# HGRN2 and mixture-of-experts trunk on one core: gate granules beside the outputs' norm, and the experts' first turning and row sums in other places

## The reference, cut to what matters

```python
def hgrn2(h, w_in, lb, o_norm_g, w_out):           # layer 1, 256 frames, 8 heads of 128
    q, f, i, g = jnp.split(h @ w_in, 4, axis=-1)
    forget = lb + (1.0 - lb) * jax.nn.sigmoid(f)
    k = 1.0 - forget;  q = jax.nn.silu(q)
    # S_t = diag(f_t) S_{t-1} + (1-f_t) i_t^T,  o_t = S_t^T q_t
    ...
    o = rms_norm(o.reshape(bsz, s, C_HEADS, C_HEAD_DIM), o_norm_g...).reshape(bsz, s, C_WIDTH)
    return (o * jax.nn.silu(g)) @ w_out

def moe_swiglu(h, w_router, b_router, w_gu, w_down):   # 8 experts, top 2, 3584 hidden
    ...
    for e in range(N_EXPERTS):
        out = out + gates[..., e:e + 1] * swiglu(h, w_gu[e], w_down[e])
    return out
```

## Time and profile before

| | us |
|---|---|
| median of 3 runs | 1519.24 |
| lowest, highest | 1518.81, 1524.04 |
| profiled execution | 1523.19 |
| its span | 1521.4 |
| PE, DVE, ACT busy in it | 1482.4, 1248.0, 1001.9 |

### The profile page before, as it was taken

One profiled execution on the slowest core, in us unless ns is written; L12 is line 12 of the kernel. 1 busy time (PEld: TensorE's weight loads), 2 busy tenths in 40 slices (PEclk: granted clock), 3 DMA queues, 4 the chain that ended last, 5 costly groups with the idle time before them and its releaser, 6 DMA issues.

```text
span 1521.4 us, 23764 instructions
## 1 busy us (share of the span) xinstructions
PE 1482.4 (97%) x6931; PEld 1231.4 (81%) x6931; DVE 1248.0 (82%) x1591; ACT 1001.9 (66%) x1267; POOL 36.3 (2%) x43
## 2 busy tenths in 40 slices
PE   8999999999988899999999999999999999999988
PEld 6877888788887688888888888888888888888876
DVE  6996545584867899988998899899989989898995
ACT  6555444375233577777877777787777778778762
POOL 1000000000000000000000000000000000000000
PEclk9999999999989999999999999999999999999999
DMA  7666655555331899999999999999999999999960
GB/s 271 214 216 220 198 189 178 177 167 184 111 111 42 281 402 386 349 376 410 336 378 410 363 349 409 381 334 411 390 324 409 405 336 386 401 348 381 410 240 28
DMA packets 124743, 453.09 MB, mean 298 GB/s; under 512 B 13968, under 2 KB 13968, under 8 KB 124704
## 3 DMA queue, kind: packets, MB, share of 16 engines
q1 hardware_dynamic: 119952, 435.25, 76.6%
q0 software_dynamic: 4752, 17.34, 3.2%
HBM read 444.14 MB, written 8.39 MB: 297 GB/s over the span
## 4 chain that ended last, share of the span: by engine, by line
PE 91%; DVE 6%; ACT 1%; issue 1%; DMA 0%; DVEq 0%; SPq 0%; ACTq 0%
PE PS L447 28%; PE PS L449 28%; PE PS L448 28%; DVE w_lo L1279 2%; PE PS L835 2%; PE PS L689 2%; DMA raw<-in_w_in_ab 0%; ACT w_hi L940 0%; DVE xT_lo L1349 0%; PE PS L497 0%; PE PS L801 0%; PE PS L515 0%; ACT xT_hi L955 0%; PE PS L583 0%; DVE x L1337 0%
## 5 line engine op out<-in xcount | busy, mean ns | idle before, releaser
L1279 DVE TENSOR_TENSOR w_lo<-raw,w_hi 128x1024 fp32r<-128x1024 f32 x486 | 568.7, 1220 | 33.2 <-ACT w_hi L940 31.0
L447 PE MATMUL PS<-w_hi,xT_hi 128*128 128x512 f32 x1424 | 566.5, 398 | 8.9 <-DVE w_lo L1279 4.0
L449 PE MATMUL PS<-w_lo,xT_hi 128*128 128x512 f32 x1424 | 557.9, 392 | 0.0
L448 PE MATMUL PS<-w_hi,xT_lo 128*128 128x512 f32 x1424 | 556.9, 391 | 0.0
L940 ACT ACTIVATE w_hi<-raw 128x1024 fp32r<-128x1024 f32 x486 | 489.6, 1061 | 71.5 <-PE PS L449 44.5
L1279 DVE TENSOR_TENSOR w_lo<-SC,w_hi 128x1024 fp32r<-128x1024 f32 x340 | 392.0, 1219 | 10.6 <-ACT w_hi L940 9.0
L940 ACT ACTIVATE w_hi<-SC 128x1024 fp32r<-128x1024 f32 x340 | 337.1, 1060 | 13.9 <-PE PS L449 9.8
L447 PEld LDWEIGHTS PS<-w_hi,xT_hi 128*128 128x128 f32 x1424 | 269.8, 189 | 63.8 <-issue 6.6
L449 PEld LDWEIGHTS PS<-w_lo,xT_hi 128*128 128x128 f32 x1424 | 268.9, 189 | 58.0
L448 PEld LDWEIGHTS PS<-w_hi,xT_lo 128*128 128x128 f32 x1424 | 269.4, 189 | 53.9
L447 PE MATMUL PS<-w_hi,hT_hi 128*128 128x512 f32 x536 | 208.9, 390 | 4.2 <-DVE hT_lo L1488 4.2
(11 more groups left out here) (261 smaller groups left out, 651.3 us busy)
## 6 DMA issues: line engine op xcount, KB each, us to landing
raw<-in_e_w_gu SPq DMA_DIRECT2D x226, 512.0 KB, 7.4
SC<-in_e_w_gu SPq DMA_DIRECT2D x222, 512.0 KB, 7.5
SC<-in_e_w_down SPq DMA_DIRECT2D x114, 512.0 KB, 7.3
raw<-in_e_w_down SPq DMA_DIRECT2D x110, 512.0 KB, 7.2
raw<-in_ffn_w_gu SPq DMA_DIRECT2D x44, 512.0 KB, 5.0
raw<-in_w_in_c SPq DMA_DIRECT2D x32, 512.0 KB, 5.6
raw<-in_ffn_w_down SPq DMA_DIRECT2D x22, 512.0 KB, 4.8
raw<-in_w_in_ab SPq DMA_DIRECT2D x20, 512.0 KB, 7.2
```

The source lines that it names most:

```text
L447: pe.matmul(out, a_hi, b_hi, start=start, stop=False, skip_group_check=True)
L448: pe.matmul(out, a_lo, b_hi, start=False, stop=False, skip_group_check=True)
L449: return pe.matmul(out, a_hi, b_lo, start=False, stop=stop, skip_group_check=True)
L1279: dve.tensor_tensor(w_lo[:, g % RING, part], raw_part(g, s), w_hi[:, g % RING, part].bitcast(F32), ALU.subtract).then_inc(lo_done, 1)
```

## The change

In the recurrence the granules of i and g come in halves: from level 2 on one half stands between two levels. Granules 14 and 15 (the second half of the gates) are moved behind the levels, around the values and the first turning. The values of tile 0 go ahead of the cross attention, in banks 4 to 7. VectorE splits one granule less at level 1 and at level 7, merges level 7 ahead of its products, and applies the gains in parts. ScalarE squares both tiles before it evaluates the second half of the gates. Ahead of q's turning stands half of granule 8.

In the expert phase, `item` has side 0 of the second unit's `unit_gu` ahead of the first turning, for all items; at item 0 the first sigmoid waits for side 0 alone (`product(G_MOE + 4)` is gone, VectorE waits for `used` instead). In the last item the gates by rank come ahead of the units (`rank_gates`), ScalarE scales the first rows, VectorE adds the second ones ahead of the last unit, `pT` is in that unit, and half of the embedding's projection stands ahead of the last down product, half behind the scattering.

```diff
@@ PE, recurrence
-            proj(8)
+            proj_part(8, 1)
+            proj_part(9, 0)
             level(0)
-            proj(9)
+            proj_part(9, 1)
+            proj_part(10, 0)
             level(1)
-            proj(10)
+            proj_part(10, 1)
             level(2)
-            proj(11)
+            proj_part(11, 0)
             level(3)
-            proj(12, (i_evac, 1))
+            proj_part(11, 1)
             level(4)
...
             level(7)
-
-            pe.wait_ge(qk_ready, 9)
...
+            proj_part(13, 1)
...
+            pe.wait_ge(i_evac, 2)
+            weigh_values(0)
+            pe.wait_ge(qk_ready, 9)
...
+            seg(G_INC + 14, 1, 0, 0, True, False)
+            weigh_values(1)
+            seg(G_INC + 15, 1, 1, 0, False, True).then_inc(gate_half, 1)
+            seg(G_INC + 14, 1, 0, 1, True, False)
...
             turn_o(0)
+            seg(G_INC + 15, 1, 1, 1, False, True)
@@ PE, item
             def item(i, last):
+                pe.wait_ge(silu_done, i * EU + (FB + 1))
+                unit_gu(G_MOE + 4, i * EU, None, (0,))
                 unit_turn(i * EU + (FB + 1))
...
-                unit_gu(G_MOE + 4, i * EU)
+                unit_gu(G_MOE + 4, i * EU, None, (1,))
                 pe.wait_ge(y_evac, i + 1)
...
                 if last:
+                    pe.wait_ge(pT_ready, 2)
+                    proj_half(1, G_MOE, 0, i * EU + EU, (0, 2))
                     pe.wait_ge(selT_ready, 1)
@@ PE, end
-            pe.wait_ge(pT_ready, 2)
-            for kk in range(2):
-                proj_half(1, G_MOE, kk, last_item * EU + EU)
+            proj_half(1, G_MOE, 1, last_item * EU + EU, (0, 2))
@@ ACT
             hi(G_MOE + 6)
-            product(G_MOE + 4)
             act.wait_ge(table_ready, 1)
@@ DVE, levels
                 dve.wait_ge(at_done, lv + 1)
+                if lv == 7:
+                    meet(7)
+                    dve.sem_inc(attn_ready, 1)
...
-                meet(lv)
-                lo(64 + lv)
...
+                    meet(lv)
+                if 1 < lv < 7:
+                    lo(63 + lv)
@@ DVE, last item
-                dve.wait_ge(y_loaded, 32)
+                dve.sem_inc(rank_ready, 1)
...
                 for t in range(T):
-                    step(dve.tensor_scalar(acc[:, t, :], acc[:, t, :], by_rank[:, 0, t:t + 1], None, ALU.mult))
+                    dve.wait_ge(acc_scaled, t + 1)
...
+                if last:
+                    rank_gates()
                 with dve.Fori(0, EU - 2) as u:
                     unit(u, False)
-                unit(EU - 2, not last)
                 if last:
-                    pT(2)
                     add_rows()
-                else:
+                unit(EU - 2, None if last else True)
+                if not last:
```

More of the change, by code:

```diff
@@ L666, in proj, with proj_part @@
                 half_granule(G_INC + n, c % 2, h, h == 0, h == 1)
+            def proj_part(n, s):
+                h = n % 2
+                pe.wait_ge(lo_done, 2 * (G_INC + n) + s + 1)
+                for t in range(T):
+                    m = part(G_INC + n, s, t, n // 2 % 2, h, h == 0, h == 1)
+                m.then_inc(used, 1)
             def turn_heads(src, signal):
@@ L738, in _ @@
                 m.then_inc(o_done, 1)
+            pe.wait_ge(i_evac, 2)
+            weigh_values(0)
+            pe.wait_ge(qk_ready, 9)
+            for hd in range(HEADS):
+                m = pe.matmul(PS[:, 6 + hd // 4, (hd % 4) * P:(hd % 4 + 1) * P], kT[:, hd, 0:P], qT[:, hd, P:SEQ],
+                              start=True, stop=True, skip_group_check=True)
+            m.then_inc(at_done, 1)
+            seg(G_INC + 14, 1, 0, 0, True, False)
+            weigh_values(1)
+            seg(G_INC + 15, 1, 1, 0, False, True).then_inc(gate_half, 1)
+            seg(G_INC + 14, 1, 0, 1, True, False)
             def turn_o(t):
@@ L811, in turn_rows, with unit_gu @@
                 m.then_inc(rows_psum, 1)
-            def unit_gu(g, turns, tokens=None):
-                for side in range(2):
+            def unit_gu(g, turns, tokens=None, sides=(0, 1)):
+                for side in sides:
                     for h in range(2):
@@ L1127, in _ @@
             by_tile(gg[:, :, 0:N], PS[:, 0:2, :], ACT.Silu, 2, g_evac)
[L1128 to L1136 removed]
+            hi(70)
+            for t in range(T):
+                act.wait_ge(qk_ready, 9)
+                act.wait_ge(o_done, t + 1)
+                act.activation(osq[t], PS[:, o_bank(t):o_bank(t) + 2, :].rearrange("p b n -> p (b n)"),
+                               ACT.Square).then_inc(o_sq, 1)
+            for t in range(T):
+                if t == 0:
+                    act.wait_ge(gate_half, 1)
+                else:
+                    product(G_INC + 16)
+                act.activation(gg[:, t, N:D], PS[:, 2 + t, :], ACT.Silu, scale=rstd(2, t)).then_inc(g_evac, 1)
+                if t == 0:
+                    hi(71)
+                    xT(0, 4, None)
+            his(72, 74)
+            xT(1, 4, None)
             def scale_x(t):
@@ L1203, in unit @@
                     unit_silu()
+                    if last and end is None:
+                        pT(2)
                     if end:
@@ L1614, in _ @@
                 ot = oo[:, t, :].rearrange("p (h n) -> p h n", n=HD)
[L1615 removed]
+                step(dve.tensor_reduce(rt[:, heads], osq[t].rearrange("p (g n) -> p g n", n=HD), AXX,
                                        ALU.add))
```

85 lines of the change are left out of this document (47 added, 38 removed).

## The result

| | us |
|---|---|
| changed, median of 5 runs | 1529.78 (1526.27 to 1530.48) |
| before, median of 5 runs beside it | 1520.61 (1518.81 to 1524.04) |
| ratio, 95% interval | 1.0054 [1.0035, 1.0073] |
| changed again, on another chip, 6 runs | 1528.55 (1525.27 to 1530.26) |
| ratio to 17 runs of before there | 1.0046 [1.0033, 1.0059] |

Slower by 0.54% and by 0.46%, 8 and 7 us. No change lies outside of both intervals, though a difference of this size is near the least that one measurement can tell. Ratios compare the means of the runs, and differences in us beside a ratio follow from it, so they are not always those of the medians. One of the 13 runs of before beside the first four experiments took 3025.84 us, in a slow state, and is in no ratio. The forecast was +6.4 and 1526.

A forecast was written before the change was run, and what follows sets the result against it. TensorE bounds the expert phase, busy for all 942.00 us; stops and low clock mark the recurrence's end. Terms -15 + 18.4 + 8.4 - 2.5 - 2.9 = +6.4 on 1519.24 gave 1526 us, likeliest 1521 to 1531, overall 1513 to 1535.

The forecast's parts named there:

- rival A: The forecast itself: late second turnings in the expert phase, most with lowered clock; 1526, range 1521 to 1531 us, chance 0.5.
- recurrence, output projection: End of the recurrence: stops removed 11.3, clock regained 5.9, late levels cost 2.9; taken as -15 us.
- item 0: First expert item: a side covers the 3.0 us stop, so the second turning comes sooner; -2.5 us.
- seven boundaries, without clock: Second turnings of items 1 to 7: TensorE waits 2.5 us at six, 3.4 at the seventh; +18.4 us.
- clock behind the stops: Expert phase: half rate costs 1.4 us behind six of eight stops, +8.4; bounds 0 and 11.2.
- tail: End of the last item: row sums leave the path, last gate's first matmul earlier; -2.9 us, bounds 0 and -6.
- The bounds 0 and 35: Range for the second turnings' stops: none late, or 5.0 us each if VectorE's slack of 2.55 were already spent.
- Rival B: Expert phase: second turnings late but no clock lost behind them; 1517 us, range 1514 to 1521, chance 0.17.
- late levels, 2.9: Recurrence: VectorE late by 1.8 us at level 4, then 0.6, 0.3, 0.2; adds 2.9 us.
- rival D: Recurrence levels become VectorE's: hand-overs cost 8 to 10 us, level 4's stop lowers the clock twice; 1532, chance 0.11.
- C: Item boundaries hide the delay because slack is larger than counted, only gains stay; 1499 us, chance 0.12.
- E: Item boundaries: late loads lengthen TensorE's stops from 2.5 to about 5 us at seven places; 1543 us, chance 0.1.

The follow-up runs named there:

- the first four experiments: Changed kernel with, in turn: first turning ahead of both sides again, 1505.84 us; 12 matmuls ahead, 1503.52; 18 matmuls ahead, 1511.86; the hidden tile sooner, 1506.62.
- the zeros' run: Changed kernel with 11 matmuls of zeros filling the stop ahead of every item's second turning: 1522.90 us, ratio 1.0004 to before.
- the item's order alone: Kernel before with only one side ahead of each item's first turning and item 0's sigmoid after the gate side: 1540.56 us, ratio 1.012.
- With zeros in that stop: Kernel before with the recurrence's part of the change and six matmuls of zeros ahead of level 4: 1506.18 us, ratio 0.9902.
- the end alone: Kernel before with only the last item's part of the change and item 0's sigmoid after the gate side: 1520.48 us, ratio 0.9992.
- the recurrence alone: Kernel before with only the recurrence's part of the change; items, row sums and projection as before: 1508.39 us, ratio 0.9917.
- 18 matmuls ahead: Changed kernel with 18 matmuls instead of 24 ahead of each item's first turning: 1511.86 us, ratio 0.9933 to before.
- 12 matmuls ahead: Changed kernel with 12 matmuls instead of 24 ahead of each item's first turning: 1503.52 us, ratio 0.9876 to before.
- the hidden tile sooner: Changed kernel with each item's first-unit hidden tile (VectorE) and sigmoid (ScalarE) ahead of granule 12: 1506.62 us, ratio 0.9899 to before.
- all together: Changed kernel with 12 matmuls ahead, rank gates just ahead of the additions, six matmuls of zeros ahead of level 4: 1502.87 us, ratio 0.9871 to before.

## Why the prediction was right, and where its terms were off

The forecast was rival A, and A is what the trace holds. By place in the two profiles of the changed kernel, each against the one of before, in us:

| | forecast | first | second |
|---|---|---|---|
| recurrence, output projection | -15 | -16.8 | -16.4 |
| item 0 | -2.5 | -0.8 | -2.4 |
| seven boundaries, without clock | +18.4 | +19.75 | +19.75 |
| clock behind the stops | +8.4 | +4.3 | +4.6 |
| tail | -2.9 | -3.4 | -3.4 |
| sum | +6.4 | +3.1 | +2.1 |

The two profiles are of the fastest runs of the changed kernel and the one of before (1523.19) is of a slower one of its own (1518.81 to 1524.04), so these sums are less than the 8 and 7 us of all runs. What the other runs of the changed kernel add, at a clock of 0.990 to 0.993, no profile places. Point by point:

- **Second turnings, +18.4.** 2.5 each and 3.4 in the last item were forecast from one subtraction. The starts give 2.50 six times, and item 0's, and 3.96 in the last: 19.0 for the seven boundaries. The turning behind a stop also takes 0.74 instead of 0.63, which with the zeros' run makes 19.75. The delay was forecast as 5.00 on VectorE and is 4.99 (7.83 for 2.84). The last item's was sized at 3.4: without the rank gates it is 2.76 (the item's order alone) and with them 1.2 more, not 0.9. The bounds 0 and 35 were far wider than needed: the slack of 2.55, counted against VectorE's delay of 5.00, is measured as 2.5. Counted against TensorE's delay of 5.45, the runs with 12, 18 and 24 matmuls give 2.95.
- **Clock behind them, +8.4.** Six of eight falls at 1.4 were forecast; the profiles show three, two of them in the 22.4 less 19.75 of the boundaries, 1.3 each, and one in the last item, 1.67, together 4.3, half of the term; the zeros give 6.4 to 7.6 by all runs. Right in sign, too dear, and wrong in its account: I had read one stop of 3.0 and one of 1.4 and put a boundary between them. The same 2.34 us stop is followed by half rate at some items and by the full clock at others. The Trainium skill, "TensorE: Matmul & The Clock Gate", section "HAM oscillation — how this bites in real kernels", describes a kernel that waits some 3 to 5 us for data in every tile and pays for the lowered clock at every one. The stops here are of 2.34 us, with one of 3.80, and three of eight pay in each profile, so the 11.2 that the prediction took from it was not what that section says of stops like these. Rival B, none of them, is excluded.
- **Recurrence, -15.** The stops went as told: outputs turned at 447.07 (448.2 forecast), no stop between the last level and the projection, the window at 1.00. The output projection starts at 450.8 (451.9 forecast, 464.67 before). Measured alone the part is -12.6, with an interval of -15.1 to -10.0. The step that was off is "late levels, 2.9", and within it two things. The lateness is 1.41 at level 4 and under 0.3 at the others, 1.7 in all, and the 1.2 by which it is short of the forecast is most of what the profile's -16.8 is over the -15. But a stop of 1.4 was taken as too short to lower the clock, by the one such row, and in five of the eight profiles with this stop it did, for 6.8 us. With zeros in that stop the part gives 14.9, near the 15. The mechanism of rival D, a stop at level 4 that costs clock, is real; its price is 2 to 3 us and not 13. How well the -15 is met can't be told closer: at the end of the recurrence of before itself the clock differs between profiles by 4.3 us (the item's order alone).
- **Item 0, -2.5.** The second turning of item 0 moved by -17.56, and the forecast for everything up to there is -17.5 (-15 and -2.5). That the two agree to 0.1 is luck: the recurrence gave 1.8 more, in a run without the fall at level 4, and item 0 gave 1.7 less. In the first profile half rate falls into item 0's work (0.72 over 490 to 496 us), in the second into matmuls of zeros beside the router, and there item 0 gives 2.4.
- **Tail, -2.9.** -3.4 in the changed kernel's profile, by the steps told: a wait of 0.62 for the scattering, 0.90 for x. Alone it is only -1.2 [-2.6, +0.2]: the step that was off is that nothing was priced behind the last gate's wait, 1.43 us before and 1.53 now, behind which the clock fell in the profile of the end alone.
- **The sum.** The parts measured alone give +18.3 - 12.6 - 1.2 = +4.5, the whole +7.0 and +8.2. Of the 2.5 to 3.7 between, 1.2 are the rank gates in the last stop; the rest is within the intervals of three comparisons. The item's order alone was expected at +25 and is +18.3, and the recurrence alone at -15 and is -12.6: the two shortfalls, one of them for the most part in the clock term, partly cancelled in the sum. So the mechanism of the forecast is shown, and that its sum came within 2 us of the measured difference is partly luck.
- **C and E.** The boundary hides 2.95 and not 5.45, so C needs half of the move. VectorE did not take weights ahead of the waiting hT_lo in 7.83 us of idle time. The Trainium skill, "TensorE: Matmul & The Clock Gate", section "Architectural detail", has the queues of these two engines in strict order, and this idle time agrees. E is excluded: every boundary's stop is released by the hidden tile and none by a load, though the DMA share is over 1 around them.

## What to carry to other kernels

To move work ahead of a step that a chain of other engines hangs on, subtract two numbers of the same trace: how long the work takes, and how long the last link of that chain had been done when it was needed. What is over is lost at each repetition; here 5.45 against a slack of 2.5 to 3. Then look for a smaller piece of the same move before giving it up, or for unneeded work ahead of the late link in its queue: half the piece cost 1.1 us in one place and kept the gain. Work that is taken out of one stop can make another: the rank gates did. And price a stop of 1.4 us or more in dense work with a share of the clock, not with all or nothing.

## What the runs showed of the hardware

- **Equal stops, unequal clock, in step.** Seven stops equal to 0.01 us, in the same instructions, were followed by half rate at two or three places. Those lie three items apart each time, with two full-rate stops between. In all, 7 of 21 such stops were followed by half rate in three profiles. TensorE at the item's order alone, three of its turnings, all of the slow kind (1.13 us):

```profile
543.56 1.13 PE L835 MATMUL PS<-ident,junk 128*128 128x128 f32 x4 [2.34 <-DVE junk L1768]
...
912.21 1.13 PE L835 MATMUL PS<-ident,junk 128*128 128x128 f32 x4 [2.34 <-DVE junk L1768]
...
1280.82 1.13 PE L835 MATMUL PS<-ident,junk 128*128 128x128 f32 x4 [2.34 <-DVE junk L1768]
```

  In the changed kernel's second profile they are 774.68 and 1143.54 (shown above), in its first 898.50 and 1267.13. The distances are 368.65, 368.61, 368.86 and 368.63, three items' length. The stops don't differ in length, so something else decides, and the places shift between executions. That it is the time at which a stop comes is a reading and not shown. The Trainium skill, "TensorE: Matmul & The Clock Gate", section "What's actually happening", says that the chip's monitor runs freely and does not start with the kernel; the shift of the places agrees with that.
- **Shorter stops.** Seven stops of 0.98 us in dense work (18 matmuls ahead) lowered the clock nowhere. Stops of 1.4 us lowered it at level 4 in five of eight profiles. At the last gate a stop of 1.43 or 1.53 stands in every kernel; the clock fell there in the end alone and with 12 matmuls ahead, and in none of the others.
- **The run-to-run spread of a kernel goes with the clock, for the most part.** Six runs of one program on one chip spread by 5.0 us, in the order of their mean granted clocks, 0.995 to 0.990. It is not the clock alone: three runs of all together took 1500.83 to 1503.26 at 0.998, and one of the filled stops 1523.53 at 0.998, where another took 1521.61 at 0.997. The versions without the items' stops still spread: four runs of each spread by 0.5 us with the hidden tile sooner, 3.2 with 12 matmuls ahead and 6.0 with all together (1500.83 at 0.998, 1506.86 at 0.995).
